# One of the four spectral products of the Hyena convolution moved from VectorE to GpSimd

## The reference, cut to what matters

```python
def long_conv_bidir(u, h, bias):
    L = u.shape[1]
    k = jnp.concatenate([h[:, 0], jnp.zeros((1, HY_WIDTH), f32), h[:0:-1, 1]], axis=0)
    k = k * lax.rsqrt(jnp.sum(k * k, axis=0, keepdims=True))
    kf = jnp.fft.rfft(k, n=2 * L, axis=0)
    uf = jnp.fft.rfft(u.astype(f32), n=2 * L, axis=1)
    y = jnp.fft.irfft(uf * kf[None], n=2 * L, axis=1)[:, :L]
    return (y + u.astype(f32) * bias.astype(f32)).astype(u.dtype)

def hyena_branch(zb, sw, sb, filt, bias):
    x0, x1, v = jnp.split(short_conv(zb, sw, sb), 3, axis=-1)
    return x0 * long_conv_bidir(x1 * v, filt, bias)
```

## Time and profile before

| what | value |
|---|---|
| median of 3 runs | 1522.93 us (1522.84 to 1524.89) |
| profiled execution, its own time | 1519.75 us |
| its span, first to last instruction | 1518.4 us |
| mean granted TensorE clock | 0.985 of full |
| PE busy | 1446.5 us, 95% of the span |
| DVE busy | 910.5 us, 60% |
| ACT busy | 678.9 us, 45% |
| POOL busy | 40.5 us, 3% |
| convolution, layer 0, first sequence | about 262 to 284 us |
| convolution, layer 0, second sequence | about 288 to 309 us |
| convolution, layer 1 | about 814 to 838 us |

### The profile page before, as it was taken

The page is one execution under the profiler, slowest core; times in us unless marked ns, Lnnn a source line. Parts: engine busy times, 40 slices in busy tenths (PEclk is TensorE's granted clock), DMA queues, the critical chain, the costliest instruction groups (busy, mean ns, idle before and its releaser), DMA issues. The chain is left out here.

```text
span 1518.4 us, 22354 instructions
## 1 busy us (share of the span) xinstructions
PE 1446.5 (95%) x9046; PEld 1236.5 (81%) x9046; DVE 910.5 (60%) x1663; ACT 678.9 (45%) x1192; POOL 40.5 (3%) x48
## 2 busy tenths in 40 slices
PE   6899999999999999989999999979999999999998
PEld 1676667778888887678788999968788889999998
DVE  5445663866424344597776776666666557766546
ACT  3533554134322233553555454556455545544434
POOL 2000000000000000100000000000000002000000
PEclk9999999999999999999999999989999999999999
DMA  8422342143322324421232555526332125555542
GB/s 316 166 97 70 138 162 75 56 163 136 111 92 89 110 84 156 145 80 60 94 134 86 204 186 184 196 79 213 133 118 79 69 84 171 190 181 181 194 170 82
DMA packets 57799, 202.53 MB, mean 133 GB/s; under 512 B 6272, under 2 KB 9536, under 8 KB 57696
## 3 DMA queue, kind: packets, MB, share of 16 engines
q1 hardware_dynamic: 55568, 194.01, 36.9%
q0 software_dynamic: 1760, 6.40, 1.2%
q10 hardware_dynamic: 368, 0.68, 0.1%
HBM read 200.02 MB, written 1.05 MB: 132 GB/s over the span
## 5 line engine op out<-in xcount | busy, mean ns | idle before, releaser
L385 PE MATMUL gemm_bank<-hhi,wlo 128*128 128x256 f32 (+1 forms) x1296 | 418.6, 323 | 17.4 <-DVE hlo L2032 4.1
L1558 DVE TENSOR_TENSOR wlo<-raw,whi 128x1024 fp32r<-128x1024 f32 x316 | 383.2, 1224 | 78.4 <-ACT whi L1068 74.6
L1068 ACT ACTIVATE whi<-raw 128x1024 fp32r<-128x1024 f32 x316 | 331.9, 1052 | 173.8 <-PE gemm_bank L387 104.3
L386 PE MATMUL gemm_bank<-hlo,whi 128*128 128x256 f32 (+1 forms) x1296 | 402.0, 310 | 0.0
L387 PE MATMUL gemm_bank<-hhi,whi 128*128 128x256 f32 (+1 forms) x1296 | 401.9, 310 | 0.0
L385 PEld LDWEIGHTS gemm_bank<-hhi,wlo 128*128 128x128 f32 x1296 | 251.3, 194 | 39.8 <-issue 22.8
L386 PEld LDWEIGHTS gemm_bank<-hlo,whi 128*128 128x128 f32 x1296 | 252.1, 195 | 11.7 <-issue 0.7
L387 PEld LDWEIGHTS gemm_bank<-hhi,whi 128*128 128x128 f32 x1296 | 251.4, 194 | 12.1
L385 PE MATMUL misc_bank<-hhi,wlo 128*128 128x256 f32 (+1 forms) x496 | 160.7, 324 | 0.0
L386 PE MATMUL misc_bank<-hlo,whi 128*128 128x256 f32 (+1 forms) x496 | 160.7, 324 | 0.0
L387 PE MATMUL misc_bank<-hhi,whi 128*128 128x256 f32 (+1 forms) x496 | 160.7, 324 | 0.0
(11 more groups left out here) (356 smaller groups left out, 1937.2 us busy)
## 6 DMA issues: line engine op xcount, KB each, us to landing
raw<-in_stream SPq DMA_DIRECT2D x364, 512.0 KB, 3.5
x<-in_x SPq DMA_DIRECT2D x1, 1024.0 KB, 6.5
x<-in_ctx SPq DMA_DIRECT2D x1, 1024.0 KB, 9.9
y<-in_hy_decay POOLq DMA_DIRECT2D x2, 512.0 KB, 5.3
arena<-in_gm_ws POOLq DMA_DIRECT2D x2, 512.0 KB, 5.7
const_b<-in_const_b POOLq DMA_DIRECT2D x1, 906.0 KB, 9.4
y<-in_hy_w POOLq DMA_DIRECT2D x2, 256.0 KB, 4.2
arena<-in_ln_g POOLq DMA_DIRECT2D x2, 256.0 KB, 2.9
```

The lines of the kernel that those rows point to most:

```text
L385: mm(out, w_lo, r_hi, start=first, stop=False)
L386: mm(out, w_hi, r_lo, start=False, stop=False)
L1068: act.activation(self.whi[:, t % SPLIT, :], self.raw[:, t % RAW, :], ACT.Copy).then_inc(*self.mark("tile_hi", "tile_hi", t))
L1558: dve.tensor_tensor(self.wlo[:, t % SPLIT, :], self.raw[:, t % RAW, :], self.whi[:, t % SPLIT, :].bitcast(F32), ALU.subtract).then_inc(*se ...
```

## The change

GpSimd computes the fourth product, im x kre, into rows 3 and 4 of `tmp`, once for each of the three convolutions, as soon as the filter (`kern`) and both splits are there. DVE no longer computes it; before the addition of the imaginary products (L1887) it waits for GpSimd's mark `cross`, and reads rows 3 and 4 of `tmp` in place of `t`. The GpSimd instructions stand in its program ahead of the wait for `conv_y` and the DMAs behind it. Nothing else moves.

```diff
             self.own(v.tensor_tensor(t, im, self.kim, ALU.mult))
             self.own(v.tensor_tensor(yre, yre, t, ALU.subtract))
-            self.own(v.tensor_tensor(t, im, self.kre, ALU.mult))
             self.dve_tiles(1)
             v.tensor_tensor(freq[:, 0, :], yre[:, 0, :], yre[:, 1, :], ALU.add)
-            self.own(v.tensor_tensor(yim, yim, t, ALU.add))
+            v.wait_ge(*self.at("cross", l, s))
+            self.own(v.tensor_tensor(yim, yim, self.tmp[:, 3:5, :], ALU.add))
...
+    def pool_conv(self, l):
+
+        for s in range(1 if l else 2):
+            self.pool.wait_ge(*self.at("kern", l, 1))
+            self.pool.wait_ge(*self.at("split", l, s, 1))
+            self.pool.tensor_tensor(self.tmp[:, 3:5, :], self.freq[:, 2:4, :], self.kre, ALU.mult).then_inc(*self.mark("pool_conv", "cross", l, s))
...
                 pool.dma_start(self.pos[:], ins["pos"]).then_inc(*self.landing("pos"))
+            self.pool_conv(l)
             pool.wait_ge(*self.at("conv_y", l, 0 if l else 1, BT - 1))
```

## The result

| | kernel before | changed kernel |
|---|---|---|
| median (range, executions) | 1523.97 us (1518.63 to 1527.55, 7) | 1530.52 us (1526.35 to 1534.55, 7) |
| ratio, 95% interval | | 1.0046 [1.0028, 1.0063] |
| profiled execution, its span | 1519.75, 1518.4 us | 1534.55, 1533.2 us |
| mean granted clock of the profiled execution | 0.985 | 0.977 |

The change makes the kernel 0.46% slower, 6.5 us between the medians. It was measured again later, beside the experiments: 1.0050 [1.0031, 1.0070]. (One of the 83 later executions of the kernel before took 1689.71 us, a slow one, and is in no mean.) The prediction had the sign and the mechanism on VectorE; it expected +4.2 us where 6.5 were measured. Its time, 1527.1 us, was 3.4 us too low: 2.3 by that difference, and 1.0 because the median of the kernel before is 1523.97 us here and was 1522.93 in the three executions it was added to.

A forecast was written before the change was run, and what follows sets the result against it. PE, 95% busy, was taken as the bound, its convolution stalls set by DVE's chain. Chain +3.0 and clock +1.2 gave +4.2 us, added to a median of 1522.93: 1527.1 us; 8-in-10 range 1522.5 to 1530.5.

The forecast's parts named there:

- DVE's chain is the path: From `split` to `spec` in all three convolutions, PE waits on DVE and gains or loses in full; 6.78 us of stall.
- The engines take turns: In each convolution, POOL's product holds one queued DVE product 2.25 us while 1.26 is saved: 0.99 us longer; chance 0.70.
- Parallel engines: Rival: POOL's and DVE's products run side by side, each of three chains loses 1.26 us: -3.8 us, 1519.1 us; chance 0.09.
- POOL last in line: Rival: queued DVE instructions keep POOL out until DVE waits for `cross`; +4.2 us, with the clock 1528.5 us; chance 0.07.
- no change: Rival: half of POOL's hold lies beside DVE work, or DVE enters partway; hold about 1.3 us, about 1523 us; chance 0.08.
- the dearer product: Rival: POOL's multiplication costs 2.94 us in each convolution; +5.0 us and one or two slow stretches, 1529.5 us; chance 0.06.
- The sum of the chain, +3.0 us: DVE's chain from `split` to `spec` gets 0.99 us longer in each of three convolutions: +3.0 us.
- The clock, +1.2 us: Behind PE's longer convolution stalls, 0.7 of one extra 1.2 GHz stretch on average, 1.7 us each: +1.2 us.
- The bound: From 0 to 3 more slow-clock stretches on PE behind the convolution stalls: 0 to +5.1 us.
- The range: The 8-in-10 range for the whole kernel's time: 1522.5 to 1530.5 us, leaving out the parallel case.

The follow-up runs named there:

- e_noprod: Kernel before with the fourth product left out on both engines, the last addition reading the third product instead: 0.9989 of the kernel before.
- e_swap_half: Changed kernel with the imaginary part first; POOL makes 512 of the fourth product's 1024 columns beside the real-part split, DVE the rest: 0.9991 of the kernel before.
- e_swap_full: Changed kernel with the imaginary part transformed, copied and split first, POOL making the whole fourth product: 1527.82 us, executed once.
- e_tile_late: Kernel before with layer 0's `wlo` tile moved from between products and combinations to behind the last combination: 0.9988 of the kernel before.
- e_fill_before: Kernel before with 6, 2 and 3 idle-filling matmuls on PE, results unused, in the stalls at the three convolutions: 1.0043 of the kernel before.

## Why the prediction was right or wrong, point by point

**DVE's chain is the path; PE gets its gains and losses in full.** Right: +0.95 of chain was +0.94 and +0.93 us of stall in layer 0 and +0.96 in layer 1. Taking 1.26 us out shortened the stall by 1.26 us (e_noprod).

**The engines take turns.** Right, with the row to the tenth: the held product at 3.42 us (said 3.4), POOL's record at 3.24 (said 3.2 to 3.4), no wait ahead of L1887, POOL in between two queued DVE instructions. Parallel engines, POOL last in line and "no change" are excluded by the trace of after itself. The multiplication cost POOL 2.40 us where nothing stood in its way (said 2.39 from additions): the dearer product is out too. Half of the 4497 ns that the Trainium skill (GPSIMD Engine Reference, section 3.1) gives for a GpSimd add of 2048 columns is an estimated 2.25 us for 1024; the trace's 2.40 is 7% more. The Trainium skill (SBUF — State Buffer, "Who interferes with whom") says that a VectorE instruction contends with a GpSimd one that reads SBUF when it has two SBUF inputs, not when it has one; both halves of that are seen here, the second in e_swap_half.

**The sum of the chain, +3.0 us.** Right: 2.9 by the traces, 3.5 (1.4 to 5.8) by time with the clock kept up.

**The clock, +1.2 us.** Wrong, and this is the step that failed. The prediction said "I expect 0.7 of one on average, because the longest stall passes 3.27 us and the others stay below 3". It measured 3.6 us by the mean clock and 3.9 and 4.5 by the two traces. It was wrong in taking the length of the stall as the test. In both profiles of the changed kernel every one of the three stalls was followed by a slow stretch, those of 2.27 and 2.74 us too, and in e_noprod one of 1.86 us was, while the kernel before went through 3.12 us at 1.00, and e_swap_full through 3.17. Counting all unfilled profiles, the convolution stalls above 3.2 us were all followed by a slow stretch, and of twelve between 1.78 and 3.17 us seven were. Length alone doesn't decide. The trace of the kernel before already hinted at it: the slow stretch 741.9 to 745.3 that the earlier trace rows uses for the price stands behind a stall of only 1.40 us.

```profile
740.17 1.13 PE L731 MATMUL misc_bank<-arena 64*128 64x512 f32 x4 [1.40 <-ACT tmp L1243]
```

So each of the three stalls should have had a chance of its own; by the counts above 2 stretches or more (3.4 us or more) was the likelier outcome, though the two rows that the prediction looked at could not give it. With 3.6 us in place of 1.2, and the chain at 2.9, the sum is 6.5 us, the measured difference; that it fits to the tenth is luck, as both differences are known only to a few us. The bound had been there (0 to +5.1 us); the value chosen inside it, and the range drawn from it, were too low. The range missed by 0.02 us.

**Profiled execution against median.** The prediction added to a median 3.2 us above the profiled execution without asking why. The profiled one had a mean clock of 0.985, the 82 later ones 0.9837 on average: by the line above that alone is 1.4 us.

**What stays open.** Why the same stall is followed by 1.2 GHz in one execution and not in another (layer 1's 1.78 us: followed by 1.00 in the kernel before, by a slow stretch in e_tile_late); why the first filled kernel before (e_fill_before) had a lower mean clock; and whether e_noprod really gains less than the 2.2 us that its profile shows.

## What to carry to other kernels

An idle GpSimd is no free second VectorE for products of two SBUF operands: here a product that takes it 2.40 us alone stopped VectorE for 2.21, and VectorE itself needs 1.22 for it. Look for a stretch in which VectorE reads PSUM, and give GpSimd as much as fits there; here that shortened the chain by 0.34 us each time, which the times alone could not resolve. Where TensorE is the bound, price a longer stall twice, once as time and once for the clock behind it; and first look for an instruction in the chain that nobody waits for yet, as the `wlo` tile here.

## What the runs showed of the hardware that was not expected

A GpSimd instruction that arrives while more VectorE instructions are queued gets in after the current one, not after the queue: 2.21 us of hold for 1024 columns in all three places. A VectorE instruction with one operand in PSUM and one in SBUF is not held at all (0.68 us beside a working GpSimd). Filling the stalls with throw-away matmuls made the changed kernel 3.7 us faster, and in its profile TensorE stayed at 2.4 GHz behind them. And 0.001 of mean granted clock goes with 1.05 us in this kernel of 1520 us; of the 2.6 us by which executions of the kernel before scatter, that line leaves 1.6.
